# A 64-byte pad ahead of the weight buffers in a two-block transformer kernel in float32r

## What is computed

```
mod  = silu(c) @ w_ada + b_ada                  # 2048 -> 6 x 2048, one row
proj = modulate(rmsnorm(x), ...) @ w_in         # 2048 -> 3904
     ... two kinds of attention, latent projections w_q_b and w_kv_b ...
x    = x + gate_m * (mixed @ w_out)             # 2048 -> 2048
h    = modulate(rmsnorm(x), ...)
x    = x + gate_f * (square(relu(h @ w_ff1)) @ w_ff2)   # 2048 -> 8192 -> 2048
```

## Time and profile before

| | us |
|---|---|
| median of 3 runs | 3133.15 |
| lowest, highest | 3132.94, 3134.68 |
| the profiled execution, its span | 3127.9 |
| PE busy (pipelined, so not the same as at its peak) | 2750.9 |
| PE's matmuls in the three products of line 1333 to 1335 | 19440 |

### The profile page before, as it was taken

One profiled execution on the slowest core, in us unless ns is written; L12 is line 12 of the kernel. 1 busy time (PEld: TensorE's weight loads), 2 busy tenths in 40 slices (PEclk: granted clock), 3 DMA queues, 4 the chain that ended last, 5 costly groups with the idle time before them and its releaser, 6 DMA issues.

```text
span 3127.9 us, 54711 instructions
## 1 busy us (share of the span) xinstructions
PE 2750.9 (88%) x21206; PEld 2647.2 (85%) x21206; DVE 2125.7 (68%) x2083; ACT 1135.3 (36%) x1269; POOL 235.3 (8%) x371
## 2 busy tenths in 40 slices
PE   2298767868999999997999986998896999999997
PEld 2287654868999999997989966998886999999997
DVE  6878763578777777777776774776767655655555
ACT  1232243323334334343334334443333434343342
POOL 7011100010000100000000000000000000000000
PEclk6599886989999999997999989999997999999998
DMA  7588720575888888784675651556773675757663
GB/s 312 229 296 287 251 81 0 172 258 181 291 273 285 288 273 287 255 283 161 194 256 172 190 173 34 181 173 212 233 242 95 195 234 174 247 182 230 200 213 124
DMA packets 299813, 658.37 MB, mean 210 GB/s; under 512 B 30689, under 2 KB 37177, under 8 KB 295225
## 3 DMA queue, kind: packets, MB, share of 16 engines
q1 hardware_dynamic: 253624, 489.07, 46.7%
q0 software_dynamic: 46080, 167.79, 17.0%
HBM read 654.69 MB, written 2.10 MB: 210 GB/s over the span
## 4 chain that ended last, share of the span: by engine, by line
PE 74%; DVE 11%; DMA 6%; issue 3%; POOL 2%; ACT 2%; SPq 0%; DVEq 0%; POOLq 0%; ACTq 0%
PE ps L1333 22%; PE ps L1335 22%; PE ps L1334 22%; DMA ada_ring<-in_w_ada 6%; DVE work L757 2%; PE ps L1540 1%; DVE work L746 1%; PE ps L1373 1%; PE ps L1374 1%; PE ps L1375 1%; PE ps L1422 1%; PE ps L1434 1%; DVE lo L732 1%; PE ps L1535 1%; PE ps L1412 1%
## 5 line engine op out<-in xcount | busy, mean ns | idle before, releaser
L732 DVE TENSOR_TENSOR lo<-raw,hi 128x1024 fp32r<-128x1024 f32 x868 | 1051.2, 1222 | 646.3 <-ACT hi L465 643.5
L465 ACT ACTIVATE hi<-raw 128x1024 fp32r<-128x1024 f32 x868 | 911.8, 1058 | 1401.6 <-PE ps L1335 1099.3
L1333 PE MATMUL ps<-acts,hi 128*128 128x256 f32 x4432 | 1276.0, 288 | 86.4 <-DVE lo L732 34.2
L1334 PE MATMUL ps<-acts,hi 128*128 128x256 f32 x4432 | 1266.3, 286 | 0.0
L1335 PE MATMUL ps<-acts,lo 128*128 128x256 f32 x4432 | 1265.9, 286 | 0.0
L1333 PEld LDWEIGHTS ps<-acts,hi 128*128 128x128 f32 x4432 | 862.1, 195 | 98.6 <-issue 49.1
L1334 PEld LDWEIGHTS ps<-acts,hi 128*128 128x128 f32 x4432 | 862.1, 195 | 2.9 <-issue 2.4
L1335 PEld LDWEIGHTS ps<-acts,lo 128*128 128x128 f32 x4432 | 861.9, 194 | 0.3
L1333 PE MATMUL ps<-f_acts,hi 128*128 128x256 f32 x2048 | 565.3, 276 | 0.0
L1334 PE MATMUL ps<-f_acts,hi 128*128 128x256 f32 x2048 | 565.3, 276 | 0.0
L1335 PE MATMUL ps<-f_acts,lo 128*128 128x256 f32 x2048 | 565.3, 276 | 0.0
(11 more groups left out here) (170 smaller groups left out, 1611.8 us busy)
## 6 DMA issues: line engine op xcount, KB each, us to landing
raw<-in_w_ff SPq DMA_DIRECT2D x512, 512.0 KB, 4.6
ada_ring<-in_w_ada POOLq DMA_DIRECT2D x320, 512.0 KB, 4.8
raw<-in_w_in SPq DMA_DIRECT2D x232, 512.0 KB, 4.6
proj<-in_w_ada SPq DMA_DIRECT2D x32, 1024.0 KB, 6.3
raw<-in_w_out SPq DMA_DIRECT2D x32, 512.0 KB, 4.9
raw<-in_w_o SPq DMA_DIRECT2D x32, 512.0 KB, 4.4
raw<-in_w_moba_out SPq DMA_DIRECT2D x16, 512.0 KB, 4.5
raw<-in_w_dsa_out SPq DMA_DIRECT2D x16, 512.0 KB, 4.5
```

The costliest lines, as they stand in the source:

```text
L465: nc.scalar.activation(hi[n % SPLIT][:, :], raw[n % RAW][:, :], ACT.Copy).then_inc(hi_ready, 1)
L732: V.tensor_tensor(lo[n % SPLIT][:, :], raw[n % RAW][:, :], hi[n % SPLIT][:, :].bitcast(F32), ALU.subtract)\
L1333: M(out, h, right[:, 0:S], start=start, stop=False)
L1334: M(out, h, right[:, S:2 * S], start=False, stop=False)
```

## The change

One buffer of 128 partitions by 16 float32, 64 bytes each, is allocated between `acts` and `raw0` and never used. No instruction is added, removed or moved. Everything allocated behind it moves up by 64 bytes: by remainder of 128, `raw`, `hi`, `lo`, `ada_ring`, `cross` and the constants go from 0 to 64, and `work`, `proj`, `y` and `f_acts` from 64 to 0. `xT` and `acts`, allocated ahead of it, stay at 0.

```diff
         xT = sb("xT", [P, KT, S])
         acts = sb("acts", [P, KT, 2 * S], F32R)
+        sb("weights_shift", [P, 16])
         raw = [sb(f"raw{i}", [P, CHUNK]) for i in range(RAW)]
         hi = [sb(f"hi{i}", [P, CHUNK], F32R) for i in range(SPLIT)]
         lo = [sb(f"lo{i}", [P, CHUNK], F32R) for i in range(SPLIT)]
```

## The result

The changed kernel takes 3080.01 us (median of 4 executions, 3076.71 to 3086.85), the kernel before 3133.91 us beside it (4 executions, 3132.94 to 3134.91). The ratio is 0.9837, with a 95% interval of 0.9822 to 0.9851. The kernel is faster, by 54 us where 72.6 us were forecast, and the time lies above the range. The profiled execution has a span of 3078.2 us against 3127.9 before, 49.7 us less.

A forecast was written before the change was run, and what follows sets the result against it. TensorE, 74% of the final chain, was taken as the bound, slowed by operand places. Terms -73.7 - 1.0 + 1.3 + 0.8 = -72.6 us took the span from 3127.9 to 3055.3 us, median 3060.5 us, range 3053 to 3073 us.

The forecast's parts named there:

- The pace of `acts`: Products with `acts` as moving operand: 120.0 to 113.4 ns each, 73.7 us off where PE's work lies on the path.
- the moving operand's own place (3174 us): Rival: a moving operand at 64 is fast, at 0 slow, so down groups lose 40.5 us; chance 0.03.
- regions (3133 us): Rival: the two paces belong to the buffers' regions of SBUF, so nothing changes; chance 0.04.
- the pair of ki2's second row tile: Products on `acts` get weights at 64 and `acts` at 0, as there: 6.6 ns off each matmul, 1.27 us a full group.
- half of it: Rival: `acts` groups gain 73 us, `f_acts` loses 40.5 as its distance from the weights changes sign: 3101 us; chance 0.02.
- Products on `f_acts`: Down groups: `f_acts` goes to 0, weights to 64, still 64 apart, so no change from 113.4 ns.
- What was late next: Waits for DVE behind a faster PE: 1.3 us lost in feed-forward first groups, 0.8 us in gates; DMA and DVE otherwise keep up.
- the clearing of `y`: DVE's 3.5 us ahead of each feed-forward's first group: the first half's gain goes into a wait, twice 0.6 = 1.3 us lost.
- The rival on the feed: PE waits for `lo` instead, up groups and gates fall 0.5 us short each, 20 us go back: about 3080 us; chance 0.05.
- The stretches bound by `ada_ring`: qk1, v1, qlat, out1: fetches and the DVE step freeing them bind, so 9 full and 2 value groups gain nothing.
- They swap: Group ki2: its first row tile becomes the fast one and its second the slow one, net nothing.
- The value groups: Operands go from same place to 64 apart: nothing taken, bounds 5 us either way for the four outside the fetch-bound stretches.

The follow-up runs named there:

- the second measurement: The changed kernel unaltered, measured again on another occasion beside the kernel before: median 3103.84 us, executions 3079.5 to 3122.3, ratio 0.9877.
- the kernel of six on a weight half: Changed kernel plus six extra matmuls, one weight half as both operands, at 16 places in feed-forwards, gates, moba and o2: 3086.09 us, ratio 0.9852.

## Why the prediction was wrong in its size

**The pace of `acts`: right in its mechanism, wrong in its value.** That two operands which differ by 64 bytes run faster than two at the same place is what the runs show, and the two rivals on the moving operand's own place (3174 us) and on regions (3133 us) fell in the runs that moved `f_acts` alone and `acts` with the weights. The step that failed is "the pair of ki2's second row tile. I take 120.0 - 113.4 = 6.6 ns off each matmul". Difference 64 has two paces, and the step took the one that the trace of before happened to show. `f_acts` was seen 32 groups long there, but always entered in the same way, from products of weights and `acts` at difference 0, and behind these it always ran at 113.4 (16 of 16). The same holds of ki2's second row tile. One entry seen eight times is one case, not eight. In the profiled execution 20 group-equivalents (gates 8, moba and dsa 4, o2 4, and parts of qk2b's 4) ran at 117.8 at least in part: gates, moba, dsa and o2 gained 6.0 us where 19.6 were forecast, qk2b 2.8 of 5.1. In qk2b each batch of the index head's small matmuls swapped the pace, so about half of its products ran at either.

The rival "half of it" had `f_acts` lose because its distance from the weights changes its sign. By 256 it does not change here: `f_acts` goes from 64 to 128 while the weights go from 128 to 192, and the difference is 64 before and after.

**Products on `f_acts`: right by luck of the execution.** "They still differ by 64: no change" held in the profile of the result (87.0 us for four down groups), and not in the second measurement (90.5). In the changed kernel down groups are no longer entered from difference 0; they inherit the pace of the up groups. That they were safe in the kernel before and are not now is a cost of the change that the prediction did not see: up to 0.85 us for each of 32 groups, 27 us.

**What was late next: right.** PE did not come to wait for DVE or DMA. In the gates there was no wait at all at 117.8 ns, and in the kernel with six extra matmuls at their start, which ran them at 113.4, each group had a pause of 0.2 us, against the 0.1 us assumed. The first groups of the two feed-forwards changed by +0.4 and -2.1 us, together -1.7, where the steps with the clearing of `y` gave twice -0.6. The rival on the feed names about the measured time (3080 us), but its mechanism, waits for `lo`, is not what the trace shows: the time came out there for another reason.

**The stretches bound by `ada_ring`: no gain, as said, but a spread that was not in the range.** The chain from 143 to 340 us is again 53.5% fetches into `ada_ring` and 17.7% line 758, as in the earlier trace rows:

```profile
by line: DMA ada_ring<-in_w_ada 53.5%; DVE work L758 17.7%; issue 13.5%; DVE lo L733 2.7%; DVE proj L935 2.5%; DVE proj L933 2.3%; DVE cross L932 2.3%; DVE acts L901 1.8%; DVE proj L907 1.6%; DVE work L764 0.9%; ACT acts L537 0.8%; POOLq L4
```

ff1's first group began at 709.2 us before and at 715.5 after. Over all the profiles of this study it began between 708.3 and 717.4 us; the changed kernel's own were 715.5, 708.3, 713.9 and 716.2, and the copy with all differences unchanged had 716.2. So these 6.3 us are within what one execution differs from another, and the profile of before happened to lie near the low end. The four profiles of the changed kernel have a mean of 713.5 us, the three kernels with `acts` at difference 0 (before, `f_acts` alone, all moved) one of 711.8. That the pad adds nothing here is likely and not shown. The 7.4 us ahead of ff1 are the second part of the miss, and their cause stays open.

**Small terms.** ki2 took 12.8 us before and after. "They swap" came true for the first row tile only. In the changed kernel its three matmuls of 128 columns all last 276 ns; of those of the second, now at difference 128, the one of line 1335 lasts 281 and the other two 276 and 274 (this in one chunk; the first chunks behind the rotation matmuls differ). First tile, 1657.75 to 1658.05 us, and second tile, 1658.42 to 1658.74 us, as in the earlier trace rows:

```profile
L1335 PE MATMUL ps<-acts,hi 128*128 128x256 f32 x1 | 0.3, 276 | 0.0
...
L1335 PE MATMUL ps<-acts,hi 128*128 128x256 f32 x1 | 0.3, 281 | 0.0
```

The value groups went from 21.8 to 22.0 us each, +0.2 within the bounds. DMA landings are as they were, 4.6 and 6.3 us.

**The best case.** Without its extra matmuls (11.4 us) the kernel of six on a weight half would have a span of 3081.9 - 11.4 = 3070.5 us, with nearly all groups at 113.4. The forecast of 3055.3 us was not to be had even then: of the 15.2 us between them 7.0 lie ahead of ff1, 3.2 in qk2b, and the others in several stages, among them 1.4 in qk2a, whose first groups ran at 117.8.

## What to carry to other kernels

Where weights are loaded anew for every matmul, compare the time of one matmul at the full clock over all stretches without waits, and the places of the two operands by remainder of 256; a pad of 64 bytes was worth 1.1 to 1.8% here, and up to 5.5% of a matmul's time. But read from a trace how each stretch was entered as well as how fast it ran, since a pace that was always entered the same way is one observation. And measure such a change over several executions on more than one occasion: here four measurements of one kernel gave gains from 1.1 to 1.8%, and the first was near the upper end.

## What the runs showed of the hardware

For a float32r matmul with 128 x 128 weights loaded anew and 256 moving columns, at a granted clock of 1.00 (2.4 GHz), start to start:

| weights less moving operand, bytes by 256 | ns |
|---|---|
| 0 | 120.0 |
| 32 | 118.3 |
| 64 | 113.4 or 117.8 |
| 96 | 117.3, 118.6 or 120.3 |
| 128 | 118.6 or 120.0 |
| 192 | 117.8, in short stretches 113.4 |

The Trainium skill's page "TensorE: Matmul & The Clock Gate" (Step-by-step: what each phase is for) has two read ports that are independent of each other. The traces do not agree in this: 5.5% of the time hangs on how the places of what the two ports read stand to each other.

At difference 64 the row of matmuls keeps the pace that it has, for as long as 31 groups (5952 matmuls), until a wait or other matmuls break it. (Where the clock fell and rose again there had been a wait of several us too, so what the clock does to the pace by itself is not shown.) Which pace follows is fixed at the tested places by the matmuls that lead in: six on one weight half to 113.4 (32 of 32), three or six on `acts` to 117.8 (16 of 16), four on one weight half or the index head's four to the other one of the two (16 of 16 and 72 of 72). Why, and what a rule for any sequence would be, stays open; so does what happens at a wait, where the runs show both outcomes.
